# Re-ordering the start, the per-chunk tail and the last tile of the RWKV stage in a two-block kernel

## The reference, cut to what matters

```
def step(state, inp):
    r_t, w_t, k_t, v_t, kk_t, b_t = inp
    sa = jnp.einsum('bhij,bhj->bhi', state, -kk_t)
    state = (state * w_t[:, :, None, :] + sa[..., None] * b_t[:, :, None, :]
             + v_t[..., None] * k_t[:, :, None, :])
    return state, jnp.einsum('bhij,bhj->bhi', state, r_t)
...
_, y = lax.scan(step, state0, xs)
mean = jnp.mean(y, axis=-1, keepdims=True)
var = jnp.mean(jnp.square(y - mean), axis=-1, keepdims=True)
y = (y - mean) * lax.rsqrt(var + GN_EPS)
y = y.reshape(bsz, seq, RWKV_WIDTH) * gn_w + gn_b
bonus = jnp.sum(r_h * k_h * r_k.astype(f32), axis=-1, keepdims=True) * v_h
y = (y + bonus.reshape(bsz, seq, RWKV_WIDTH)) * g
...
x = x + g_m * (concat(y_r, y_m) @ w_out)
```

## Time and profile before

| | before |
|---|---|
| median of 3 runs | 1850.59 us (1850.32 to 1851.39) |
| the profiled execution | 1851.39 us |
| its span | 1849.7 us |
| PE busy | 1735.3 us (94%) |
| DVE busy | 991.7 us (54%) |
| POOL busy | 828.3 us (45%) |
| ACT busy | 574.3 us (31%) |
| chain that ended last | PE 69%, DMA 10%, DVE 7%, POOL 6%, issue 5%, ACT 3% |

### The profile page before, as it was taken

One profiled execution on the slowest core, in us unless ns is written; L12 is line 12 of the kernel. 1 busy time (PEld: TensorE's weight loads), 2 busy tenths in 40 slices (PEclk: granted clock), 3 DMA queues, 4 the chain that ended last, 5 costly groups with the idle time before them and its releaser, 6 DMA issues.

```text
span 1849.7 us, 26709 instructions
## 1 busy us (share of the span) xinstructions
PE 1735.3 (94%) x10754; PEld 1271.5 (69%) x10754; DVE 991.7 (54%) x1367; ACT 574.3 (31%) x1031; POOL 828.3 (45%) x401
## 2 busy tenths in 40 slices
PE   6999889898997778999999999999999899999998
PEld 4868578777332324777777777777777688888887
DVE  6696688543111115567878789466889712222112
ACT  4342733533322214333545544643000210001000
POOL 0442256341111103243322232236988687887884
PEclk8999999999999999999999999999999999999999
DMA  8822135455999994222221222123565232332331
GB/s 297 319 100 92 57 105 153 150 205 183 396 419 419 420 412 183 75 90 81 68 80 58 81 69 69 59 67 114 195 217 216 84 103 92 99 93 92 102 103 69
DMA packets 68374, 290.65 MB, mean 157 GB/s; under 512 B 9632, under 2 KB 9632, under 8 KB 55840
## 3 DMA queue, kind: packets, MB, share of 16 engines
q1 hardware_dynamic: 61488, 271.65, 41.0%
q10 hardware_dynamic: 2160, 8.91, 1.2%
q0 software_dynamic: 4608, 8.40, 1.2%
HBM read 282.37 MB, written 14.94 MB: 161 GB/s over the span
## 4 chain that ended last, share of the span: by engine, by line
PE 69%; DMA 10%; DVE 7%; POOL 6%; issue 5%; ACT 3%; POOLq 0%; ACTq 0%; DVEq 0%; SPq 0%
PE bank L2864 67%; DMA arena<-weights_dram 8%; POOL hi_ring L2835 2%; POOL lo_ring L2837 2%; PE bank L2868 2%; DVE arena L2413 1%; POOL lo_ring L2811 1%; ACT arena L2239 1%; DVE late L3417 1%; DMA arena<-mod_weights_dram 0%; DVE arena L3417 0%; DMA xT<-x_dram 0%; DVE arena L1869 0%; DVE merged_lo L2608 0%; DVE arena L2730 0%
## 5 line engine op out<-in xcount | busy, mean ns | idle before, releaser
L2864 PE MATMUL bank<-h_lo,hi_ring 128*128 128x512 f32 x648 | 255.7, 395 | 0.0
L3552 POOL TENSOR_TENSOR lo_ring<-ring,hi_ring 128x1024 fp32r<-128x1024 f32 x46 | 118.9, 2586 | 245.2 <-ACT hi_ring L2805 245.2
L2864 PE MATMUL bank<-arena 64*64 64x64 f32 (+5 forms) x1704 | 193.3, 363 | 36.4 <-DMA arena<-weights_dram 31.7
L2864 PE MATMUL bank<-mix_h_hi,lo_ring 128*128 128x512 f32 x576 | 227.4, 395 | 0.0
L2837 POOL TENSOR_TENSOR lo_ring<-ring,hi_ring 128x1024 fp32r<-128x1024 f32 x77 | 207.3, 2692 | 6.0
L2835 POOL TENSOR_TENSOR hi_ring<-ring,col 128x1024 fp32r<-128x1024 f32 x77 | 159.3, 2069 | 62.9 <-PE bank L2864 62.3
L2864 PEld LDWEIGHTS bank<-arena 128*64 128x64 f32 (+2 forms) x1704 | 97.8, 146 | 119.1 <-issue 106.9
L2864 PE MATMUL bank<-mix_h_hi,hi_ring 128*128 128x512 f32 x416 | 166.4, 400 | 4.2 <-ACT con L2321 1.5
L2413 DVE SCALAR_TENSOR_TENSOR arena<-bank,col,arena 128x511 f32<-128x511 f32 (+14 forms) x240 | 156.6, 726 | 0.0
L2864 PEld LDWEIGHTS bank<-h_lo,hi_ring 128*128 128x128 f32 x648 | 121.7, 188 | 29.2
L2864 PE MATMUL bank<-ffn_h_hi,lo_ring 128*128 128x512 f32 x352 | 138.2, 392 | 0.0
(11 more groups left out here) (464 smaller groups left out, 3975.1 us busy)
## 6 DMA issues: line engine op xcount, KB each, us to landing
ring<-weights_dram SPq DMA_DIRECT2D x200, 512.0 KB, 3.5
arena<-weights_dram SPq DMA_DIRECT2D x61, 1024.0 KB, 25.0
arena<-mod_weights_dram SPq DMA_DIRECT2D x54, 512.0 KB, 4.8
late<-mod_weights_dram SPq DMA_DIRECT2D x42, 512.0 KB, 3.6
ring<-weights_dram SPq DMA_DIRECT2D x15, 1024.0 KB, 28.6
hT<-weights_dram SPq DMA_DIRECT2D x10, 1024.0 KB, 29.0
late<-weights_dram SPq DMA_DIRECT2D x5, 1024.0 KB, 28.7
xT<-x_dram SPq DMA_DIRECT2D x4, 1024.0 KB, 6.6
```

The source lines that it names most:

```text
L2864: return pe.matmul(out, lhsT, rhs, start=start, stop=stop, skip_group_check=True)
L3552: pool.tensor_tensor(ring_r[:, u % RING, :], ring[:, u % RING, :], hi_unit(u).bitcast(F32), ALU.subtract).then_inc(S("split"), 1)
```

## The change: what it does

Five edits, all in the RWKV stage.

1. Start. On PE `corrected(0)`, `corrected(1)` come first, then `decayed_keys(0)`; `corrected(2)` moves into chunk 0 behind `y`'s state part, `corrected(3)` to chunk 0 behind the rest of `y`, `decayed_keys(1)` into chunk 1. ACT's copies follow in the same order. The table load moves from step 4 of the inverse to the head of this stage.
2. DVE's gate work at c = 1: the four multiplications of `gate_r` by `gn_w` (L1299) are gone; the one on `bonus` (L1296) stays.
3. In DVE's chunk loop `half_add(0, c-3)` moves from the head of the chunk to behind the state's update.
4. ACT's `rate_out` of an odd chunk goes ahead of `upper`, and POOL's `lower_out(2)` goes from the middle of its tile 0 to the head of its tile 1, where it stands behind the lower part of tile 0.
5. Last tile: DVE multiplies y, `gn_w` and gate ahead of time into a new area `gn_gated` (four instructions 128x128), and one pair of multiplications falls away behind ACT's last Exp.

```diff
--- before
+++ after
@@ -727,2 +727,3 @@
         gn_square, gn_rate = area(4128, RW, P), area(4640, RW, P)
+        gn_gated = area(5152, RW, P)
         silu_c2 = area(12384, D)
@@ -941,10 +942,6 @@
+            corrected(0)
+            corrected(1)
             pe.wait_ge(*at_count("r_tok", 2 * TT))
-            for k in range(2):
-                for x in range(2):
-                    pe.wait_ge(*at_count("inv", n_level(5, k, x)))
             decayed_keys(0)
-            for k in range(4):
-                corrected(k)
-            decayed_keys(1)
             pe.wait_ge(*at_count("r_tok", 4 * TT))
@@ -968,2 +965,6 @@
                 last.then_inc(S("y_state_done"), 1)
+                if c == 0:
+                    corrected(2)
+                if c == 1:
+                    decayed_keys(1)
                 if c >= 2:
@@ -984,2 +985,4 @@
                 last.then_inc(S("y_in_done"), 1)
+                if c == 0:
+                    corrected(3)
                 if c >= 2 and half == 0:
@@ -1076,4 +1079,2 @@
                     product(1 + (s + 1) // 4, (s + 1) % 4)
-                if s == 4:
-                    act.preload_act_table_set(LN_EXP)
                 if 8 <= s < 16 and s % 2:
@@ -1120,4 +1121,4 @@
+            act.preload_act_table_set(LN_EXP)
             act.wait_ge(*at_count("mod_used", MOD_OUT))
-            decayed_keys(0, 0)
             corrected(0)
@@ -1125,12 +1126,16 @@
             act.wait_ge(*at_count("r_tok", 4 * TT))
+            decayed_keys(0, 0)
             second_values(0)
             decayed_keys(0, 1)
-            corrected(2)
-            corrected(3)
             second_values(1)
-            decayed_keys(1, 0)
-            decayed_keys(1, 1)
             for c in range(2 * TT):
+                if c == 0:
+                    corrected(2)
+                if c == 1:
+                    decayed_keys(1, 0)
+                    decayed_keys(1, 1)
                 act.wait_ge(*at_count("y_in_done", c + 1))
                 act.activation(y_rwkv[:, :, c * C64:c * C64 + C64], four(bank[at[("y", c)]][:, 0:256]), ACT.Copy).then_inc(S("y_raw"), 1)
+                if c == 0:
+                    corrected(3)
                 if c < 2:
@@ -1147,6 +1152,6 @@
                     square(c // 2 - 1)
-                if c >= 5 and c % 2:
-                    upper(c // 2 - 2)
                 if c >= 3 and c % 2:
                     rate_out(c // 2 - 1)
+                if c >= 5 and c % 2:
+                    upper(c // 2 - 2)
             square(TT - 1)
@@ -1276,4 +1281,2 @@
                 other = half_rows(1 - half)
-                if c >= 3:
-                    half_add(0, c - 3)
                 if half == 0:
@@ -1296,5 +1299,4 @@
                     steps.mark(dve.tensor_tensor(bonus[:, :, 3 * P:4 * P], bonus[:, :, 3 * P:4 * P], gate_r[:, :, 3 * P:4 * P], ALU.mult))
-                    steps.wait()
-                    for n in range(RW):
-                        steps.mark(dve.tensor_scalar(gate_r[:, n, 3 * P:4 * P], gate_r[:, n, 3 * P:4 * P], column("rwkv_gn_w", n), None, ALU.mult))
+                if c >= 3:
+                    half_add(0, c - 3)
                 if c >= 4 and half == 0:
@@ -1307,11 +1309,11 @@
             scaled(tt - 1)
+            dve.wait_ge(*at_count("gn_centred", TT))
+            for n in range(RW):
+                steps.mark(dve.scalar_tensor_tensor(gn_gated[:, n, :], y[:, n, :], column("rwkv_gn_w", n), gate_r[:, n, tt * P:tt * P + P], ALU.mult, ALU.mult))
             half_add(0, 5)
-            for half in range(2):
-                by_n = last_rate(half).rearrange("p (n t) -> p n t", n=2)
-                dve.wait_ge(*at_count("gn_std", TT + half))
-                steps.mark(dve.tensor_tensor(by_n, by_n, gate_r[:, 2 * half:2 * half + 2, tt * P:tt * P + P], ALU.mult))
             steps.wait()
             for half in range(2):
-                by_n = last_rate(half).rearrange("p (n t) -> p n t", n=2)
-                steps.mark(dve.tensor_tensor(by_n, by_n, y[:, 2 * half:2 * half + 2, :], ALU.mult))
+                dve.wait_ge(*at_count("gn_std", TT + half))
+                two = gn_gated[:, 2 * half:2 * half + 2, :].rearrange("p n t -> p (n t)")
+                steps.mark(dve.tensor_tensor(last_rate(half), last_rate(half), two, ALU.mult))
             steps.wait()
@@ -1350,2 +1352,4 @@
                 y = y_rwkv[:, :, tt * P:tt * P + P]
+                if tt == 1:
+                    lower_out(2)
                 pool.wait_ge(*at_count("gn_scaled", tt + 1))
@@ -1354,3 +1358,4 @@
                 pool.tensor_tensor(y, y, gate_r[:, :, tt * P:tt * P + P], ALU.mult).then_inc(S("y_rwkv"), 1)
-                lower_out(2 + tt)
+                if tt:
+                    lower_out(2 + tt)
                 pool.wait_ge(*at_count("y_hi", MH + tt + 1 if tt < TT - 2 else MH + TT + 1))
```

More of the change, by code:

```diff
@@ L1147, in act_rwkv @@
                     square(c // 2 - 1)
+                if c >= 3 and c % 2:
+                    rate_out(c // 2 - 1)
                 if c >= 5 and c % 2:
                     upper(c // 2 - 2)
-                if c >= 3 and c % 2:
-                    rate_out(c // 2 - 1)
             square(TT - 1)
```

## The result

The changed kernel takes 1864.55 us (median; 1850.89 for the kernel before), a ratio of 1.0078 [1.0051, 1.0104]: slower, by 0.8%, and by more than forecast. The prediction was 1855.4 with a range up to 1858.5. One of its runs, at 2445.94 us with a mean granted clock of 0.651, is left out. Timed again on another chip the kernel took 1865.09 against 1852.98, 1.0081 [1.0055, 1.0106].

A forecast was written before the change was run, and what follows sets the result against it. PE bounds: it waits for others in chunks 0 to 2, never idles in 3 to 7. Minus 2.9, minus 1.6, plus 5.0, plus 2.7, plus 1.6 give plus 4.8: 1856.2 profiled, median 1855.4 us, range 1849.5 to 1858.5.

The forecast's parts named there:

- Last tile: End of the stage: about 0.8 us off the chain behind ACT's last Exp, but PE is busy, so nothing won or lost.
- The start: Chunks 0 to 2: minus 2.9 us from the earlier start and shorter waits, minus 1.6 from the low clock going.
- the idle that preceded it is gone, so minus 1.6: Chunk 2 from `new_state` to the next `ws`: low clock gone, minus 1.6 us; at worst nothing.
- The wait on `x_half`: Chunks 3 to 6: the group's sum waits 1.25 us for the later `half_add`, four times, plus 5.0 us.
- The wait on `split`: Chunk 6: `out_half(0, 4)` waits for the later `lower_out(2)`, plus 2.7 us, bounds 0 to 3.0.
- The low clock behind it: PE's clock falls once, in chunk 6 or before chunk 0: plus 1.6 us, bounds 0 and 3.2.
- (a): Rival: only one of the waits on `x_half` and `split` binds, 1851.1 or 1850.4 us; chance 0.18.
- (b): Rival: neither wait binds in chunks 3 to 7, only the start's gain is left, 1846.1 us; chance 0.10.
- (d): Rival: both new waits bind and no low clock follows, 1853.8 us; chance 0.15.
- (c): Rival: worse start, low clock before chunk 0 too or the table load's drain real, 1857 to 1858 us; chance 0.12.

The follow-up runs named there:

- edit 5 alone: Against the start alone: last tile done with `gn_gated` as in the changed kernel, no gate multiplications in chunk 3; 1852.68 us, ratio 1.0000.
- the start alone: Changed kernel keeping only the new order of `corrected` and `decayed_keys`, table load in the inverse, gate multiplications in chunk 3; 1848.94 us, ratio 0.9979 to the kernel before.

## Why the prediction was wrong, point by point

**The step that failed** is "Last tile", in the sentence "`gn_gated` fits in the wait for the last Exp". The sum put the four instructions, and all of the last tile, at nothing and gave no bounds; only run alone, in some 1.1 us, do they fit in the 1.94 us before the first product. They took 5.42 us, the lower part of the last tile began 11.28 us after `centred` did (405.77 to 417.05) and not 8.14 (396.06 to 404.20), the tensor engine waited 2.78 us for it, and its clock fell during the wait and stayed low for 6.8 us: 5.38 us in all. With this one edit undone the two pieces took 5.55 us again, as before. "But PE is busy through that time" was true only while the chain of the last tile stayed shorter than PE's work; 3.1 us more made it the longer one. The rows needed stood in the prediction itself. It had found that four small multiplications (the 2.86 us in the earlier trace rows) stand still while GpSimd works, and did not ask what GpSimd does where four more of them were put. It starts on tile 2 as soon as `scaled` ends, that is, within 0.15 us of `gn_gated` (408.64 and 408.49).

**The start**, -3.03 instead of -4.5. The table load was right: 1.28 us, the next activation 0.02 behind it, 1.1 to 1.3 us by the two pairs of kernels. The Trainium skill (ScalarE: Activation LUTs, What ACT_TABLE_LOAD costs) adds a drain of about 1.38 us; the trace does not agree, 346.83 plus 1.28 and then 348.13. The stall of the gate multiplications is gone as said. What failed is "the idle that preceded it is gone, so minus 1.6": of the twelve profiles with the new start, chunk 2 took 6.17 to 6.22 in six and 7.66 to 8.74 in the other six, and in two of the first six the low clock stood in chunk 0 instead. Only four of the twelve ran chunks 0 to 2 without it. A break of 1.24 us inside `new_state` of chunk 1, with no semaphore, is new as well; chunk 1 took 5.16 where 4.5 was forecast.

**The wait on `x_half`** was right in cause, place and size: 1.18 us in chunks 3 to 5, and 5.05 for the four in the kernel that has it alone, forecast 5.0.

**The wait on `split`** was right: 2.45 us, forecast 2.7. **The low clock behind it** was in the right place and too small. It cost 1.6 alone, as priced, and about 2.9 in both profiles of the changed kernel (12.32 less 6.19, 2.45 and 0.79), where it lasted 6.8 us instead of 3.4 and the 0.79 us wait on `x_half` lay inside the slow stretch. In two kernels with the same two waits (table load back, edit 5 undone) the slow stretch lasted 3.4 us, was over or nearly so when the `x_half` wait came, and cost 1.4 and 1.5. So the two waits by themselves don't make 2.9; that it takes the second inside the slow stretch fits these four profiles and was not tested. The sum had the low clock once, at 1.6; in the first profile it fell three times, in the second four times.

**Rivals.** (a), (b) and (d) fell: both waits bound and the clock fell. (c) held in part: in the second profile the low clock came in chunk 0 too, and the drain is not there. The rival that would have been the answer, GpSimd against the new vector work at the end, was not among them, and so the range ended 6 us too low. Of the miss of 7.4 us in the stage, 5.4 is the last tile, 1.5 the start, 0.6 chunk 6. In chunk 6 two errors partly cancel: waits of 3.24 against 3.95 forecast, and a low clock of 2.9 against 1.6. The median missed by 9.15; what lies outside the stage varies by some us without any edit.

## What to carry to other kernels

Work put "into a wait" of the vector engine has to be priced by what GpSimd does in that very stretch, and the first thing to look up is what releases GpSimd: here the instruction right before the new ones. Small instructions are no protection: three of the four were each held for one GpSimd operation. Where an operation that frees a PSUM bank is moved behind other work, its new end against the matmul that takes the bank, times the chunks, gives the cost to a tenth. And an edit that only brings one part of the change can be the gain: here the new order at the start, with the gate work away from `lower_out(1)`, was worth 5.6 us of the stage, while moving `half_add` (5.1), edit 4 (4.1 in chunk 6), the work at the end (4.2) and the table load (1.1 to 1.3) each cost something by themselves.

## What the runs showed of the hardware

Four SCALAR_TENSOR_TENSOR of 128x128 with both tensors in SBUF took 1.1 us alone and 5.42 beside back-to-back GpSimd TENSOR_TENSOR, in both kernels that were looked at closely, three of the four being held for one GpSimd operation each; GpSimd's own times hardly changed (1.32 and 1.30 us, against 1.28 and 1.29 before). Vector instructions that read a bank of PSUM were not held in that way: the product pair at 400.83 took 0.76 us beside the `lower_out` of 400.48 (before), and 0.75 at 414.49 with GpSimd idle.

The low clock came with single idle stretches of 2.45 and 2.78 us of the tensor engine, in the last tile also with those of 1.62 and 1.63 (the kernels with edit 5 alone and with edit 4 undone), and not behind those of 1.18. Idle stretches of 1.9 to 2.2 us before chunk 0 were followed by it in three of six profiles. In chunk 2 it came in half of the profiles with much the same pattern of work (it came behind a break of 1.24 us in the changed kernel and not behind one of 1.32 in the start alone). What decides it in these two places stays open.

The break inside `new_state` of chunk 1, always behind its fifteenth matmul record, 0.23 to 2.15 us, shows no semaphore. It appeared in eleven of the twelve profiles with the new order at the start and in neither of the kernel before. In all eleven a packet of the DMA queue marked "instruction" (q8) ended 1.3 to 1.6 us before the tensor engine went on (356.32 and 357.65 in the changed kernel). That fits a wait for instructions to arrive; no run tested it.
